# Linear attention in a fused network: its tables and rank weights loaded a layer ahead, the positions a layer later

## What is computed

```python
def gla_mixer(x, w_in, w_gate_up, b_gate, norm_g, w_out):
    q, k, v, r, g_lr = jnp.split(x @ w_in, GLA_SPLITS, axis=-1)
    log_a = jax.nn.log_sigmoid((g_lr @ w_gate_up + b_gate).astype(jnp.float32)) / GLA_TAU
...
def second_block(x, p, positions, ...):
    ang = positions.astype(jnp.float32)[..., None] * inv_freq
    cos, sin = jnp.cos(ang), jnp.sin(ang)
    for i in range(DEPTH_2):
...
        x = layer_norm(ALPHA * x + h, ln_g[i, 0], ln_b[i, 0])
        x = layer_norm(ALPHA * x + sq_relu_mlp(x, mlp_w1[i], mlp_w2[i]), ln_g[i, 1], ln_b[i, 1])
        x = x + jax.nn.sigmoid(x @ ple_w_gate[i]) * (p[i] @ ple_w_proj[i])
```

## Time and profile before

| | |
|---|---|
| median of three runs | 3235.81 us (3231.53 to 3239.92) |
| the profiled execution | 3227.11 us, its span 3225.1 us |
| TensorE (PE) busy | 3058.5 us, 95% of the span |
| weight loads of TensorE (PEld) | 2734.1 us, 85% |
| VectorE (DVE) | 1672.0 us, 52% |
| ScalarE (ACT) | 1366.3 us, 42% |
| POOL | 233.5 us, 7% |
| transfers | 477.09 MB, 148 GB/s over the span |

### The profile page before, as it was taken

How to read it: one execution, slowest core, us unless ns; L and a number is a source line. 1 busy time by engine, 2 the same in 40 slices (tenths; PEclk the granted TensorE clock), 3 DMA queues, 4 the chain that set the end, 5 groups by cost and what they waited for, 6 DMA issues and landing times. The chain is left out here.

```text
span 3225.1 us, 55686 instructions
## 1 busy us (share of the span) xinstructions
PE 3058.5 (95%) x22904; PEld 2734.1 (85%) x22904; DVE 1672.0 (52%) x2530; ACT 1366.3 (42%) x2146; POOL 233.5 (7%) x328
## 2 busy tenths in 40 slices
PE   7999999999999999998889789998999999989998
PEld 5777788777778887788789789998899999978998
DVE  4322355453223532235765457666665686556765
ACT  4222242542223422224455355546553565354644
POOL 1111124201100000002300000000000000000000
PEclk9999999999999999999999899999899999999999
DMA  7555543325544223425245543544255445543553
GB/s 266 182 164 183 171 145 120 105 94 177 172 132 142 93 89 123 125 92 141 71 149 184 165 131 120 194 157 151 92 189 190 161 159 186 188 135 118 169 185 105
DMA packets 406673, 477.09 MB, mean 148 GB/s; under 512 B 11180, under 2 KB 383484, under 8 KB 406474
## 3 DMA queue, kind: packets, MB, share of 16 engines
q1 hardware_dynamic: 380176, 389.05, 37.2%
q0 software_dynamic: 25440, 84.91, 8.4%
q10 hardware_dynamic: 858, 0.29, 0.0%
HBM read 470.91 MB, written 4.84 MB: 148 GB/s over the span
## 5 line engine op out<-in xcount | busy, mean ns | idle before, releaser
L447 DVE TENSOR_TENSOR w_lo<-w_raw,w_hi 128x1024 fp32r<-128x1024 f32 x734 | 896.4, 1227 | 1186.6 <-ACT w_hi L444 1185.5
L455 PE MATMUL bank<-a_hi,w_hi 128*128 128x256 f32 (+1 forms) x3992 | 1265.0, 317 | 51.4 <-DVE a_lo L2295 15.2
L456 PE MATMUL bank<-a_lo,w_hi 128*128 128x256 f32 (+1 forms) x3992 | 1250.0, 313 | 0.0
L457 PE MATMUL bank<-a_hi,w_lo 128*128 128x256 f32 (+1 forms) x3992 | 1249.0, 313 | 0.0
L444 ACT ACTIVATE w_hi<-w_raw 128x1024 fp32r<-128x1024 f32 x734 | 769.6, 1056 | 948.7 <-PE bank L457 929.5
L455 PEld LDWEIGHTS bank<-a_hi,w_hi 128*128 128x128 f32 x3992 | 766.8, 192 | 117.3 <-issue 67.5
L456 PEld LDWEIGHTS bank<-a_lo,w_hi 128*128 128x128 f32 x3992 | 768.0, 192 | 43.4
L457 PEld LDWEIGHTS bank<-a_hi,w_lo 128*128 128x128 f32 x3992 | 765.8, 192 | 45.0
L455 PE MATMUL bank<-h_hi,w_hi 128*128 128x256 f32 (+1 forms) x1824 | 566.5, 311 | 0.0
L457 PE MATMUL bank<-h_hi,w_lo 128*128 128x256 f32 (+1 forms) x1824 | 559.9, 307 | 0.0
L456 PE MATMUL bank<-h_lo,w_hi 128*128 128x256 f32 (+1 forms) x1824 | 559.7, 307 | 0.0
(11 more groups left out here) (326 smaller groups left out, 2237.6 us busy)
## 6 DMA issues: line engine op xcount, KB each, us to landing
w_raw<-in_mlp_w SPq DMA_DIRECT2D x128, 1024.0 KB, 5.2
w_raw<-in_w_ffn_gate_up SPq DMA_DIRECT2D x88, 1024.0 KB, 5.2
m_raw<-in_w_mod POOLq DMA_DIRECT2D x104, 512.0 KB, 4.8
w_raw<-in_w_ffn_down SPq DMA_DIRECT2D x32, 1024.0 KB, 5.3
w_raw<-in_gla_w_in SPq DMA_DIRECT2D x24, 1024.0 KB, 5.4
w_raw<-in_w_in SPq DMA_DIRECT2D x16, 1024.0 KB, 6.2
w_raw<-in_ple_w_gate SPq DMA_DIRECT2D x16, 1024.0 KB, 5.1
w_raw<-in_w_ffn_down SPq DMA_DIRECT2D x16, 768.0 KB, 5.6
```

What stands on the lines that cost most here:

```text
L447: e.tensor_tensor(w_l, raw, w_h.bitcast(F32), ALU.subtract).then_inc(S.lo_ready.sem, 1)
L455: e.matmul(dst, hi, rhs_hi, start=start, stop=False)
L456: e.matmul(dst, hi, rhs_lo, start=False, stop=False)
L457: return e.matmul(dst, lo, rhs_hi, start=False, stop=stop)
```

## The change

The seven loads and two clearings of a GLA layer become a function of their own, `gla_tables(j)`, called a layer ahead: for layer 0 after the first block's last mixer (`mix(1, True, None)`) and ahead of `ffn_last`, for layer 3 after the MLP of layer 2 and ahead of its PLE. It notes the count of transfers in `at.tables`, and the two waits in `decays` (TensorE's ahead of the rank product, VectorE's ahead of the scan) wait for that count. The five tiles lie together behind 16 x 512 + 22 x 256 floats of the region, in the part of `h_lo` that the last FFN does not use. The positions and frequencies move behind layer 0's mixer, into `mla_positions`, with a wait for all transfers ahead of their border.

```diff
             g_end = sb("g_end", [P, GLA_HEADS * 4], F32, h)
             g_rank = sb("g_rank", [P, T], F32, h)
+        with ExitStack() as h:
+
+            sb("region_h_5", [P, 16 * TT + FT * T], F32, h)
+            w_glr = sb("w_glr", [P, DK, P // 4], F32, h)
             w_gate = sb("w_gate", [P, GLA_HEADS * P], F32, h)
+            g_low = sb("g_low", [P, P], F32, h)
+            g_up = sb("g_up", [P, P], F32, h)
+            g_carry = sb("g_carry", [P, GLA_HEADS * T], F32, h)
...
-            def gla(j, i):
+            def gla_tables(j):
 
                 w = A["gla_w_in_2"][j]
                 if pool:
                     side_wait()
                     border()
                     e.memset(w_glr[:, :, :], 0.0).then_inc(S.pool.sem, 1)
...
                     side_load(dst[:, :], C[name][:])
+                at.tables = at.side
+
+            def tables_wait():
+                e.wait_ge(side_sem, at.tables)
+
+            def gla(j, i):
+
+                w = A["gla_w_in_2"][j]
...
                     if pe:
-                        side_wait()
+                        tables_wait()
...
                     if dve:
-                        side_wait()
+                        tables_wait()
...
+            def mla_positions():
+
+                if pool:
+                    side_wait()
+                    border()
+                pos = A["positions_2"]
+                side_load(pos_i[:, :], bass.AP(tensor=pos.tensor, offset=pos.offset, ap=[[0, P], [1, T]]))
+                side_load(freq[:, :], C["mla_freq"][:])
+
...
                 yield mix(1, True, None)
+                gla_tables(0)
                 yield ffn_last(1, 1)
-                if pool:
-                    border()
-                pos = A["positions_2"]
-                side_load(pos_i[:, :], bass.AP(tensor=pos.tensor, offset=pos.offset, ap=[[0, P], [1, T]]))
-                side_load(freq[:, :], C["mla_freq"][:])
                 for i in range(DEPTH_2):
...
                     if i == 0:
+                        mla_positions()
                         at.beside = mla_angles()
                     yield mlp(i)
                     at.beside = None
+                    if i == 2:
+                        gla_tables(1)
                     yield ple(i)
```

More of the change, by code:

```diff
@@ L321, in build @@
             state = sb("state", [P, GLA_HEADS, GLA_DV], F32, h)
-            w_glr = sb("w_glr", [P, DK, P // 4], F32, h)
             g_end = sb("g_end", [P, GLA_HEADS * 4], F32, h)
             g_rank = sb("g_rank", [P, T], F32, h)
+        with ExitStack() as h:
+            sb("region_h_5", [P, 16 * TT + FT * T], F32, h)
+            w_glr = sb("w_glr", [P, DK, P // 4], F32, h)
             w_gate = sb("w_gate", [P, GLA_HEADS * P], F32, h)
+            g_low = sb("g_low", [P, P], F32, h)
+            g_up = sb("g_up", [P, P], F32, h)
+            g_carry = sb("g_carry", [P, GLA_HEADS * T], F32, h)
         with ExitStack() as h:
@@ L328, in build @@
             r_gate = sb("r_gate", [P, DK, T], F32, h)
-            g_low = sb("g_low", [P, P], F32, h)
-            g_up = sb("g_up", [P, P], F32, h)
-            g_carry = sb("g_carry", [P, GLA_HEADS * T], F32, h)
         with ExitStack() as h:
```

## The result

The changed kernel took 3207.82 us in the median of five runs (3202.19 to 3214.65), the kernel before 3235.81 (3231.53 to 3239.92): a ratio of 0.9921, 95% interval 0.9904 to 0.9938, or 20 to 31 us less. The forecast was 3218.0. The profiled executions lie closer together: 3207.82 against 3227.11 us, 19.3 less, where the sum promised 17.8. Which of the two differences is the change's own is what the first experiments ask. Means over several runs leave out three executions of over 3290 us; all others lie between 3198 and 3246 us.

What follows compares the result with a forecast made beforehand. TensorE's waits for g_carry, the last small load, in layers 0 and 3, with half clock behind them, were the bound. 11.64 + 6.20 = 17.8 us off 3227.11 gives 3209.3, plus 8.7 for the median: 3218.0; range 3209 to 3230.

Steps and rivals of the forecast that it cites:

- the sum: Gains of layers 0 and 3 together: 11.64 + 6.20 = 17.8 us, taking the profiled 3227.11 to 3209.3 us.
- Tables ahead: Linear attention layers: TensorE's rank product no longer waits for g_carry; gain 11.64 us in layer 0, 6.20 in layer 3.
- What is late next: Ahead of the p_in transposes: VectorE's g_rank copy, behind a weight cut, comes late and leaves TensorE a 2.2 us gap.
- The clock falls anyway: Rival, chance 0.15: the remaining 2.2 us TensorE gap halves the clock, 1.2 us more lost per layer; 3222.7 us.
- T: Follow-up theory: VectorE work lengthening TensorE's stop costs each layer 2.45 us plus some 1.5 to 2 us of half clock.
- Tables at their new places: Behind the first block's last mixer and layer 2's MLP: moved loads cost 0, landing 9.84 us after the first clearing.
- The port lock: POOL's clearings beside VectorE: a shared exclusive port could cost VectorE up to 2 x 0.83 us, leaving 16.1; 0 was taken.
- `p_in` and the positions: p_in lands 5.4 and 8.3 us before need; positions behind layer 0 are first read some 90 us later; cost 0.
- The starting point: Base of the forecast: the three runs' median, 3235.8, stood 8.7 us above the profiled 3227.11, giving 3218.0.
- tables late in layer 3: Rival, chance 0.04: POOL's loads are held up beside busy VectorE, layer 3's gain is lost; 3224.2 us.
- another wait: Rival, chance 0.03: p_in, not the tables, bound TensorE, so nothing is won; 3235.8 us.
- weight tiles behind the tables: Rival, chance 0.04: at the new places weight tiles wait behind the tables, 39.4 us lost against 17.8; 3257.4 us.

Runs made afterwards that it cites:

- the first experiments: Both kernels run again without an edit: the kernel before against itself, ratio 0.9991; the changed kernel against the kernel before, 0.9948.
- layer 0 only: Changed kernel with layer 3's tables loaded inside layer 3 again, layer 0's still ahead; run twice, 0.9951 and 0.9949 of the kernel before.
- layer 3 only: Changed kernel with layer 0's tables loaded inside layer 0 again, layer 3's still ahead, positions behind layer 0; 0.9956 of the kernel before.
- later rank product: Changed kernel with the rank product one weight tile later, behind the first k pair; 0.9952 of the kernel before.
- third and fourth changed runs: The changed kernel without an edit, run again in two other jobs; 0.9932 and 0.9930 of the kernel before.
- tables twice: Changed kernel with the seven small loads made twice at each new place, the second time behind the first's landing; 0.9924 of the kernel before.
- longer stop: Changed kernel with two unneeded VectorE multiplications ahead of the g_rank copy; one execution, layer 0 159.0 us, layer 3 175.4 us.

## Why the prediction was right, and where it was off

**Tables ahead, 11.64 and 6.20: right.** The six traces with layer 0's tables ahead (layer 0 only twice, changed four times) have a mean of 154.3 us for layer 0, 12.4 below the 166.7 of the kernel before. The four changed runs and layer 3 only have 172.1 for layer 3, 5.8 below the mean of 177.9 of the five with its tables inside. Before rounding that is 18.1 together, against 17.8. That layer 0 gave 0.7 us more and layer 3 0.4 less was not traced; in the sum the two largely cancel. The steps came as told: the rank product 1.07 us (0.97 foretold), the copy behind the cut, a stop of 2.06 us (2.2), transposes to product 1839.93 - 1839.54 = 0.39 (0.38).

**What is late next: told only in part.** The copy ends the stop, as foretold. The prediction did not name the wait behind the layer's last `w_in` product, which hangs on the decays (line 2589; 2.3 us in layer 0 before too). It is why the stop of 2.06 us could not be had by a later rank product: that wait and those for `v_g` grew by 1.6 and 0.9 us per layer, and the layers became longer.

**The clock falls anyway (0.15): it can, in layer 3.** In the profiled execution of the changed kernel the clock stayed full behind both stops. In its second profile, layer 3 shows full clock at the stop and half behind it:

```profile
2860.00:2862.00 2.00, 0.01 (x1) 0.04 (x1) 1.56 (x2) 0.30 (x1) 0.00 (x0) 1.00 0.73 260
2862.60:2866.00 3.40, 3.40 (x20) 3.40 (x19) 0.76 (x2) 0.50 (x2) 0.00 (x0) 0.54 0.95 296
```

It came with layer 3 only as well, and not in the third and fourth changed runs or with the tables twice, with the same stop of 2.06 us each time: in two of six profiles in layer 3, and in none of seven in layer 0. Yet it costs the layer nothing that can be seen (172.4 us with and without), for in all four profiles where the clock stays up behind the stop, it was down at the layer's entry instead, and in the other two it was up there. The changed kernel's window there, in the profile first read:

```profile
2837.80:2841.00 3.20, 3.20 (x17) 3.20 (x17) 1.83 (x6) 0.34 (x2) 0.72 (x1) 0.51 0.89 268
```

So the rival's mechanism exists, and its price of 1.2 us a layer does not show among these profiles: it moves a loss rather than adding one. But the sum was read from a profile whose clock was full at layer 3's entry, and so has the loss at neither place; whether the 0.4 us that layer 3 fell short of 6.20 are part of it was not told apart. The stop on line 2589 shows too that one length of stop can go either way: behind its 2.24 and 2.44 us the clock fell in both layers of the profile first read, and in neither layer of the next three profiles. The loss at the entry also bears on T's size in the longer stop's layer 3, whose entry was at full clock.

**Tables at their new places, 0: right.** With the tables twice the first round had landed 8.8 us behind its first clearing in layer 0's place (1637.13 - 1628.32) and 10.2 in layer 3's, where 9.84 was foretold, and twice the loads cost nothing that can be seen. The first block ends at 1820.70 us, before at 1821.07. The port lock that might have cost up to 1.66 us did not show: POOL's clearing at 1626.89 ran beside a VectorE row, the one at 2817.44 met another at its end, and both rows took what they take elsewhere. VectorE, changed kernel:

```profile
1626.96 0.55 DVE L970 RECIPROCAL r_tmp<-r_tmp 128x64 f32<-128x64 f32 x1 [1.42 <-ACT r_tmp L966]
...
2817.86 1.23 DVE L450 TENSOR_TENSOR w_lo<-w_raw,w_hi 128x1024 fp32r<-128x1024 f32 x1 [0.87 <-ACT w_hi L447]
```

The clearings took 0.31 and 0.53 us, in the old place 0.30 and 0.52. The prediction was wrong that VectorE was idle in the old places and that no row shows the two side by side: in layer 0 the cut at 1839.06 ran beside both clearings and took its usual 1.23 us, so this could have been read before. By the Trainium skill (SBUF — State Buffer, "Who interferes with whom") only certain VectorE forms take the shared ports; the trace agrees in that neither these rows nor the clearings took longer for running side by side.

**`p_in` and the positions, 0: right.** No wait for either is shown on TensorE; the positions went out at 1976.31, behind the layer.

**The starting point: off.** The sum set the profiled execution at 3227.11 - 17.8 = 3209.3, which is the mean of the 29 executions. To the tenth that is luck: the profiled execution lay 1.4 us below its kernel's mean, and the difference of the means is 1.4 above the sum. The forecast then added 8.7 us, to stand against a median of three runs. That median was high: the mean of 93 executions is 3228.5, 1.4 above the profiled one. This step, not a term of the sum, made 3218.0 out of 3209.3, and put the lower end of the range, 3209, above the median that was measured, 3207.82.

**The remaining rivals** (tables late in layer 3, another wait, weight tiles behind the tables) needed a wait for a transfer, and in the two layers of the changed kernel none is shown.

## What to carry to other kernels

A stop of TensorE is priced by the place where the same work stands again at full clock: waiting time, plus what the half clock behind it adds, minus the stop that the next late thing leaves. Before chasing that remaining stop, look for the next wait of the same stage that hangs on the same chain of work: here it takes back what a later rank product saves, and shrinks with an earlier one. A difference of 10 us between two medians of a few runs is not to be explained from the trace before the kernel has been run against itself.

## What the runs showed of the hardware

**Two paces at full clock.** The same loop of matmuls runs at one of two paces while the granted clock is 1.00, and which one changes from execution to execution. One window, four executions (the count behind PE busy is of matmuls): before and changed, 1660 to 1740 us, then the changed kernel's second and third profiles:

```profile
1660.00:1740.00 80.00, 80.00 (x709) 80.00 (x708) 46.72 (x58) 40.40 (x61) 0.00 (x0) 1.00 0.59 194
```

```profile
1660.00:1740.00 80.00, 80.00 (x708) 80.00 (x708) 46.73 (x58) 40.39 (x61) 0.00 (x0) 1.00 0.59 195
```

```profile
1660.00:1740.00 80.00, 80.00 (x682) 80.00 (x680) 44.87 (x58) 39.09 (x58) 0.00 (x0) 1.00 0.57 184
```

```profile
1660.00:1740.00 80.00, 80.00 (x682) 80.00 (x681) 44.80 (x58) 39.20 (x57) 0.00 (x0) 1.00 0.57 187
```

80 us by 709 is 112.8 ns a matmul, by 682 it is 117.3: 4%, kept through the whole loop, and some 3 us in each 80. The kernel before does it too: from 2680 to 2720 it ran x342, and in its second profile x355. Matmuls missing from the trace do not explain it, for the work itself takes longer: from POOL's first clearing to the `fac` row the two slower executions need 199.7 and 198.5 us, the first and fourth of the changed kernel 194.1 and 193.4. What sets the pace was not found.

**The clock falls inside attention.** In layer 1's attention, far from the change, TensorE counts as busy nearly all the time (23.5 of 24 us in the first row), and yet its clock fell in some executions. Windows over nearly the same work, kernel before, before again, changed, changed a third time:

```profile
2258.00:2282.00 24.00, 23.54 (x98) 15.77 (x98) 12.53 (x34) 9.40 (x36) 0.00 (x0) 0.79 0.00 1
```

```profile
2258.00:2289.00 31.00, 30.53 (x97) 19.45 (x98) 12.63 (x35) 9.37 (x35) 0.00 (x0) 0.61 0.00 0
```

```profile
2246.00:2267.00 21.00, 20.53 (x104) 13.28 (x103) 13.46 (x36) 9.82 (x36) 0.00 (x0) 1.00 0.00 0
```

```profile
2251.00:2282.50 31.50, 31.03 (x101) 19.90 (x101) 12.93 (x35) 9.47 (x36) 0.00 (x0) 0.62 0.00 1
```

Some 3 to 11 us hang on it. From VectorE's first row with `mask_m` to its last `a_lo` row of this stage it is 26.3 us in ten profiles, 31.0 and 37.1 in the two of the kernel before. The third profile of the changed kernel, 3220.88 us, has 37.2, so it lost 10.9 us here, and 3 in each 80 us of the loop above, against the fourth's 3203.28. By the Trainium skill (TensorE: Matmul & The Clock Gate, "What's actually happening") the clock's changes keep a time of their own that does not start with the kernel; the runs agree as far as the same work at the same place had full clock in one execution and half in the next. Both profiles of the kernel before fell here, and of twelve others only two (the third of the changed kernel and, by 3 us, the later rank product).

The mean granted clock of each execution says how often. The profiles with the long fall have 0.969 and 0.973; the changed kernel's other three have 0.977 or 0.978. Of the 88 executions of the kernel before for which it was kept, 22 had 0.972 or less, of the 29 changed ones 3 had 0.973 or less. Without these the means are 3225.8 and 3208.1 us, 17.7 apart, close to the sum, and the 3217.4 us of layer 3 only lie 8.4 below the first, close to the 7.6 of its two layers. So about 1.5 of the 19.2 us go with the share of executions at a lower clock. The bounds were set with the results in view, and whether the change moves the odds, 22 of 88 against 3 of 29, is not settled by so few.
